# Loading and splitting weights in two phases of a one-core hybrid decoder step

## The chip, the cores and the metric

The kernel runs on one core of one Trainium2 chip. The metric is the device time of one execution in microseconds (us). Three runs of the kernel before took 3761.02, 3762.74 and 3765.28 us, so the median is 3762.74 us.

Engine names in the profile: PE is the matrix engine (PEld its weight loads), DVE the vector engine, ACT the scalar engine, POOL the general engine; SP issues the DMAs that matter here, and SPq is its queue. A time such as 2690.67 is in microseconds from the first instruction of the profiled execution.

## The reference

One layer of a decoder. A prompt of 4096 tokens and 32 sample tokens (8 sequences of 4) are normalised and projected by `w_in` into a pooling group (`u`, gate) and an attention group (q, k, v, gate, forget logits). The part that matters here is what stands behind attention:

```python
z = jnp.einsum('btd,de->bte', h, w_in_l)            # u_pool, g_pool, q, k, v, g_attn, logits
...
outs.append((end[..., sl] - start) / cnt - uf[..., sl])   # mean over 2, 4, 8, 16 tokens, minus the token
mixed = jnp.einsum('btgc,gcd->btgd', pooled, pool_w_l) * pool_scale_l
...
mix = jnp.concatenate([pool_out * jax.nn.silu(g_pool),
                       attn_out.reshape(b, t, ATTN_W) * jax.nn.silu(g_attn)], axis=-1)
return x + jnp.einsum('bte,ed->btd', mix, w_out_l)  # then a final RMSNorm
```

Everything is float32. A product of two float32 matrices is made of three matmuls: each operand is split into a high part, which is a rounded copy, and a low part, which is the operand minus that copy, and high x high, high x low and low x high are added up in PSUM.

## The kernel before, in words

Five phases follow each other, each with its own buffers and semaphores and with a barrier of all engines between them: project, decode (attention of the sample tokens over the cache), attend (prompt), gates (`phase_gates`, L1093) and merge (`phase_merge`, L1419). The change touches the last two.

**Gates** computes `u` and the two gates, for 512 prompt tokens (a super tile) at a time, eight times. First it needs its weights: 8 chunks of 128 rows x 1536 columns (`w_in`, 768 KB each in two DMAs). SP loads a chunk into one of two raw slots, which lie in the buffer of the later output stage (L1177, L1178). ACT scales it by the norm weight and rounds it to `w_high` (L1236), DVE makes `w_low` (L1278), and that frees the slot for the chunk after the next. PE multiplies each finished chunk with the 32 sample tokens (three columns of 512, three passes: 9 matmuls a chunk, 72 in all). Behind chunk 1 SP also issues the first `h_t` (2 MB, the tokens of the first super tile), the pooling weights, the history and `den`.

Behind the last chunk stands the sample chain: DVE inverts `den` (L1282) and splits the pooling weights; ACT copies and applies the sigmoid to the sample results (L1240, L1242); PE makes 8 small matmuls for the pooled sample tokens (L1381, L1382), DVE copies them, PE makes 4 more (L1386, 8 records in the trace), and DVE multiplies the gates (L1304 to L1308). Then DVE splits the first `h_t` into `h_high` and `h_low` in 8 chunks (L1292, L1293), and PE begins the first super tile.

A super tile has 12 groups of output columns (u = 0 to 11), each of 8 chunks x 3 passes = 24 matmuls of 128x128 by 512; ACT evacuates or applies a sigmoid, DVE makes sums, gates and the next `h_t` split. Three PSUM banks `acc` rotate over the groups. Group u = 11 closes a super tile; DVE then splits the next `h_t`, and PE waits for its first chunk. All eight super tiles are one loop on PE (`Fori`).

**Merge** loads `w_out` in 8 chunks of 128 x 1024 (512 KB, L1494) into two raw slots; DVE alone rounds (L1558) and subtracts (L1559). Behind chunk 1 stand the sample's inputs and `norm_row`. PE turns the sample's mix around, multiplies it chunk by chunk (6 matmuls a chunk, 48 in all) into `acc`, and DVE adds and normalises it (L1598, L1600). SP issues behind the last weight chunk the first half super tile of inputs (`load_mix(0, 0)`: four loads of 512 KB and two of 256 KB, L1480 and L1482), then x (1 MB), then the same for the second half. DVE joins the inputs and splits them (`split_mix`, L1575 to L1581). PE waits until DVE has added the sample result (`s_done` 2) before it starts the loop over eight super tiles of four token tiles t, 48 matmuls each. In the loop SP loads the mix for half b of the next super tile when DVE has freed the buffer, but in program order behind the store of y and the load of x of the other half.

## Time and profile before

| what | us |
|---|---|
| median of three runs | 3762.74 |
| the profiled execution's own time | 3761.75 |
| its span, first to last instruction | 3760.2 |
| PE busy in the span | 3457.5 (92%) |
| from 2680, end of attend, to the first matmul of the first super tile of gates | 55.6 |
| one super tile of gates | 76 |
| from the last transpose of gates (3341.4) to the first token tile of merge | 51.9 |

The profiled execution is one run of its own; its time stands 1.0 us below the median of the three. The page's busy shares are means over phases with different limits, so the stretches in question are read by themselves from the timeline. A figure in square brackets at the end of a timeline row is how long that engine had been idle, and what it waited for.

### The profile page before, as it was taken

The numbers are of one execution on the slowest core, as the hardware profiler recorded it, in microseconds if no ns is written. First come the engines' busy times: TensorE is split into PE (matmuls) and PEld (weight loads), VectorE is DVE, ScalarE is ACT, GpSimd is POOL, SyncE is SP. The second block draws the span as 40 slices with busy tenths as digits, with TensorE's granted clock in tenths as the row PEclk, the third lists the DMA queues.
The fourth block names the chain that finished last, engine by engine and source line by source line (L and its number), as shares of the span: only waits on it lengthen the run. The fifth ranks groups of instructions, "written<-read, shape, count | busy, mean of one in ns | idle before, by whom it ended". The sixth has DMA issues, their size and how long they took to land. (4 is left out here: it accounts for less than half of the span.)

```text
span 3760.2 us, 51171 instructions
## 1 busy us (share of the span) xinstructions
PE 3457.5 (92%) x18808; PEld 2382.5 (63%) x18808; DVE 1709.7 (45%) x2714; ACT 1176.0 (31%) x1611; POOL 1198.2 (32%) x1145
## 2 busy tenths in 40 slices
PE   7999999797948999999999999999799999979998
PEld 5777777573715555655565656565377777757887
DVE  3222221262526655555555555555243444445554
ACT  4221121141314455555555555554301000000100
POOL 0000000134324666666666666666400000000000
PEclk9999999897978999999999999999899999989999
DMA  4222232499983020202020212100311111136765
GB/s 149 90 101 101 103 121 81 159 347 388 335 303 73 18 54 21 57 23 57 23 57 23 55 25 52 29 21 9 103 49 67 45 56 56 45 110 185 212 209 163
DMA packets 216028, 392.73 MB, mean 104 GB/s; under 512 B 60135, under 2 KB 102120, under 8 KB 213775
## 3 DMA queue, kind: packets, MB, share of 16 engines
q1 hardware_dynamic: 195079, 322.22, 27.6%
q0 software_dynamic: 20768, 68.17, 4.8%
q8 instruction: 105, 1.72, 0.2%
q14 instruction: 76, 0.62, 0.0%
HBM read 288.50 MB, written 101.99 MB: 104 GB/s over the span
## 5 line engine op out<-in xcount | busy, mean ns | idle before, releaser
L928 DVE TENSOR_REDUCE at_max_parts<-at_mx 128x1 f32<-128x512 f32 (+3 forms) x1152 | 731.0, 645 | 494.9 <-PE at_mx L997 425.4
L802 POOL TENSOR_TENSOR at_pair_sum<-at_probs 128x1024 f32<-128x1024 f32 x224 | 532.0, 2375 | 424.3 <-ACT at_probs L852 424.3
L852 ACT ACTIVATE at_probs<-at_st,at_gap 128x1024 f32<-128x1024 f32 x448 | 498.0, 1113 | 523.1 <-PE at_st L1029 516.2
L1049 PE MATMUL at_o_ps<-at_probs,at_v 128*64 128x512 f32 (+3 forms) x2304 | 541.8, 581 | 0.0
L1028 PE MATMUL at_st<-at_q_all,at_k_all 128*128 128x512 f32 (+3 forms) x1152 | 476.4, 414 | 0.0
L997 PE MATMUL at_mx<-at_k_one,at_q_top 67*128 67x512 f32 (+3 forms) x1152 | 453.5, 395 | 8.7 <-DVE at_max_parts L928 5.9
L1029 PE MATMUL at_st<-at_q_one,at_k_one 67*128 67x512 f32 (+3 forms) x1152 | 439.2, 381 | 0.0
L1028 PEld LDWEIGHTS at_st<-at_q_all,at_k_all 128*128 128x128 f32 x1152 | 217.8, 189 | 224.6 <-ACT at_probs L852 115.2
L93 PE MATMUL ga_acc<-ga_h_high,ga_w_high 128*128 128x512 f32 x768 | 312.0, 406 | 22.9 <-DVE ga_h_low L1293 21.3
L95 PE MATMUL ga_acc<-ga_h_high,ga_w_low 128*128 128x512 f32 x768 | 308.4, 402 | 0.0
L94 PE MATMUL ga_acc<-ga_h_low,ga_w_high 128*128 128x512 f32 x768 | 308.3, 401 | 0.0
L803 POOL TENSOR_TENSOR at_quad_sum<-at_pair_sum 128x512 f32<-128x512 f32 x224 | 287.8, 1285 | 17.6
L1049 PEld LDWEIGHTS at_o_ps<-at_probs,at_v 128*64 128x64 f32 x2304 | 146.3, 138 | 208.5 <-issue 156.8
L997 PEld LDWEIGHTS at_mx<-at_k_one,at_q_top 67*128 67x128 f32 x1152 | 219.7, 191 | 64.8 <-DVE at_max_parts L928 17.1
L1029 PEld LDWEIGHTS at_st<-at_q_one,at_k_one 67*128 67x128 f32 x1152 | 220.4, 191 | 30.2
L93 PE MATMUL mg_acc<-mg_w_high,mg_mix_high 128*128 128x512 f32 x512 | 201.0, 393 | 22.0 <-DVE mg_xs L1598 17.1
L93 PE MATMUL pj_acc<-pj_h_high,pj_w_high 128*128 128x512 f32 x512 | 209.6, 409 | 6.2 <-DVE pj_fs L430 6.2
L1522 POOL MEMSET mg_minus_half<- 128x1 f32 x1 | 0.1, 99 | 656.0 <-POOLq L66 656.0
L95 PE MATMUL pj_acc<-pj_h_high,pj_w_low 128*128 128x512 f32 x512 | 206.1, 403 | 0.0
L94 PE MATMUL pj_acc<-pj_h_low,pj_w_high 128*128 128x512 f32 x512 | 205.6, 402 | 0.0
L94 PE MATMUL mg_acc<-mg_w_low,mg_mix_high 128*128 128x512 f32 x512 | 200.4, 391 | 0.0
L95 PE MATMUL mg_acc<-mg_w_high,mg_mix_low 128*128 128x512 f32 x512 | 200.1, 391 | 0.0
(305 smaller groups left out, 4926.1 us busy)
## 6 DMA issues: line engine op xcount, KB each, us to landing
dc_pages<-in_cache_k_dram SPq DMA_DIRECT2D x128, 256.0 KB, 5.2
dc_pages<-in_cache_k_dram POOLq DMA_DIRECT2D x128, 256.0 KB, 5.2
dc_pages<-in_cache_v_dram SPq DMA_DIRECT2D x128, 256.0 KB, 7.1
dc_pages<-in_cache_v_dram POOLq DMA_DIRECT2D x128, 256.0 KB, 5.4
pj_x<-in_x_prompt_dram SPq DMA_DIRECT2D x32, 512.0 KB, 3.8
scratch_h_t<-pj_h_t SPq DMA_DIRECT2D x8, 2048.0 KB, 10.1
at_q_raw<-scratch_q_t SPq DMA_DIRECT2D x128, 128.0 KB, 3.0
at_k_raw<-scratch_k_t SPq DMA_DIRECT2D x64, 256.0 KB, 4.1
```

The lines of the kernel that those rows point to most:

```text
L93: nc.tensor.matmul(out, lhs_high, rhs_high, start=first, stop=False)
L94: nc.tensor.matmul(out, lhs_high, rhs_low, start=False, stop=False)
L95: return nc.tensor.matmul(out, lhs_low, rhs_high, start=False, stop=last)
L802: chain.link(nc.gpsimd.tensor_tensor(pair, first, second, ALU.add))
L803: nc.gpsimd.tensor_tensor(out, pair[:, 0], pair[:, 1], ALU.add).then_inc(summed, 1)
L852: nc.scalar.activation(probs[:, s % RING], st[:, s % 2], ACT.Exp, bias=bias).then_inc(exp_done, 1)
L928: nc.vector.tensor_reduce(max_parts[:, b % AHEAD, t, c:c + 1], mx[:, bank_of["unit", k] % 2, 0:width], AX_X, ALU.max).then_inc(bank_done, 1)
L997: last = nc.tensor.matmul(mx[:, n % 2, 0:width], q_top[0:KR, b % AHEAD, t * P:(t + 1) * P], k_one[h % 2][0:KR, c * TILE:c * TILE + width], ...
L1028: nc.tensor.matmul(out, k_all[h % 2][:, keys], q_all[:, b % AHEAD, at:TILE], start=True, stop=False)
L1029: last = nc.tensor.matmul(out, k_one[h % 2][0:KR, keys], q_one[0:KR, b % 2, at:TILE], start=False, stop=(c < j))
L1049: last = nc.tensor.matmul(o_ps[half * HD:(half + 1) * HD, b % 2, at:TILE], v[:, h % 2, 4 * c + own], probs[:, s % RING, half, at:TILE], st ...
L1522: nc.gpsimd.memset(minus_half[:], -0.5)
```

## The change

In gates there are four raw slots in place of two: three in a larger stage buffer, one in `u_t`. `norm_col` and `den` are loaded first, then the weights, with `h_t` behind chunk 5 and the other constants behind chunk 7. The inversion of `den` stands ahead of the weights on DVE. ACT makes the first `h_high` (8 copies) behind the last `w_high`, DVE only the subtractions. The sample's projections go to a PSUM tile `side` of their own, and the rest of the sample chain moves into the first super tile, which is now written out ahead of the loop: the 8 small matmuls ahead of u = 10, the 4 others behind u = 11, DVE's part between its gates.

In merge all eight chunks have a slot of their own, ACT rounds them and DVE subtracts. `load_mix(0, 0)` is issued behind chunk 4 and `norm_row` behind chunk 7; DVE runs `split_mix(0, 0)` between chunks 4 and 5. The sample's result goes to the other `acc` buffer, and PE waits for its addition only ahead of t = 1 of the first super tile, written out too.

```diff
--- before.py
+++ after.py
...
-INVERTED = 7
+INVERTED = 3
+PW_SPLIT = 9
 BANDS_READY = 10
-LAST_COPY = 15
+LAST_COPY = 13
...
+    WSLOTS = 4
...
+        stage = m.sb("stage", [P, 2 * CH + 2, TILE])
+        pool_stage, gate_stage, sig = stage[:, 0:CH], stage[:, CH:2 * CH], stage[:, 2 * CH:2 * CH + 2]
...
+        w_raw = [flat[:, 0:NW], flat[:, NW:2 * NW], flat[:, 2 * NW:3 * NW], u_t[:].rearrange("p c t -> p (c t)")[:, 0:NW]]
...
+        side = m.ps("side", [P, 3, W])
+        s_acc, s_mixed, last_ps = side[0:NS], side[0:NS, 0], side[0:HIST, 1]
+        s_ps = side[:, 0, 0:CH * NS].rearrange("p (g t) -> p g t", g=CH)
...
+            sp.dma_start(norm_col[:], io["norm_w"].rearrange("l (c p) -> p (l c)", p=P), allow_slow_non_contiguous=True).then_inc(norm_loaded, 16)
+            sp.dma_start(den, io["den"].rearrange("h (a t) -> (h a) t", t=DEN)).then_inc(den_loaded, 16)
+            for c in range(KC):
+                if c >= WSLOTS:
+                    sp.wait_ge(w_low_dve, c - WSLOTS + 1)
+                rows = w_in[c * P:(c + 1) * P]
+                slot = w_raw[c % WSLOTS]
+                sp.dma_start(slot[:, 0:2 * W], rows[:, U0:U0 + 2 * W]).then_inc(w_loaded[c % WSLOTS], 16)
+                sp.dma_start(slot[:, 2 * W:NW], rows[:, GA0:GA0 + W]).then_inc(w_loaded[c % WSLOTS], 16)
+                if c == 5:
+                    sp.dma_start(h_t[:], io["h_t"][0]).then_inc(h_loaded, 16)
+            sp.dma_start(pw_raw[:], io["pool_w"].rearrange("l g c d -> c (l g) d")).then_inc(const_loaded, 16)
+            sp.dma_start(hist[:], io["state_pool"].rearrange("l b i c -> (l b i) c")).then_inc(const_loaded, 16)
             sp.dma_start(scale_col[:], io["pool_scale"].rearrange("l (c p) -> p (l c)", p=P), allow_slow_non_contiguous=True).then_inc(const_loaded, 16)
             sp.dma_start(scale_row[:], io["pool_scale"].to_broadcast([NS, W])).then_inc(const_loaded, 16)
-            for c in range(KC):
-                if c >= 2:
-                    sp.wait_ge(w_low_dve, c - 1)
-                rows = w_in[c * P:(c + 1) * P]
-                slot = w_raw[:, (c % 2) * NW:(c % 2 + 1) * NW]
-                sp.dma_start(slot[:, 0:2 * W], rows[:, U0:U0 + 2 * W]).then_inc(w_loaded[c % 2], 16)
-                sp.dma_start(slot[:, 2 * W:NW], rows[:, GA0:GA0 + W]).then_inc(w_loaded[c % 2], 16)
-                if c == 1:
-                    sp.dma_start(h_t[:], io["h_t"][0]).then_inc(h_loaded, 16)
-                    sp.dma_start(pw_raw[:], io["pool_w"].rearrange("l g c d -> c (l g) d")).then_inc(const_loaded, 16)
-                    sp.dma_start(hist[:], io["state_pool"].rearrange("l b i c -> (l b i) c")).then_inc(const_loaded, 16)
-                    sp.dma_start(den, io["den"].rearrange("h (a t) -> (h a) t", t=DEN)).then_inc(den_loaded, 16)
             sp.wait_ge(setup, INVERTED)
             sp.dma_start(io["inv_den"].rearrange("h (a t) -> (h a) t", t=DEN), den).then_inc(inv_stored, 16)
...
+            act.wait_ge(norm_loaded, 16)
             for c in range(KC):
-                act.wait_ge(w_loaded[c % 2], 32 * (c // 2 + 1))
-                nc.scalar.activation(w_high[:, c], w_raw[:, (c % 2) * NW:(c % 2 + 1) * NW], ACT.Copy, scale=norm_col[:, c:c + 1]).then_inc(w_high_ready, 1)
+                act.wait_ge(w_loaded[c % WSLOTS], 32 * (c // WSLOTS + 1))
+                nc.scalar.activation(w_high[:, c], w_raw[c % WSLOTS], ACT.Copy, scale=norm_col[:, c:c + 1]).then_inc(w_high_ready, 1)
+            act.wait_ge(h_loaded, 16)
+            for c in range(KC):
+                nc.scalar.activation(h_high[:, c], h_t[:, c], ACT.Copy).then_inc(h_high_first, 1)
...
             dve.wait_ge(den_loaded, 16)
             link(nc.vector.reciprocal(den, den))
             assert n_setup[0] == INVERTED
-            dve.wait_ge(const_loaded, 80)
+            dve.wait_ge(norm_loaded, 16)
+            for c in range(KC):
+                dve.wait_ge(w_high_ready, c + 1)
+                nc.vector.scalar_tensor_tensor(out=w_low[:, c], in0=w_raw[c % WSLOTS], scalar=norm_col[:, c:c + 1],
+                                               in1=w_high[:, c].bitcast(F32), op0=ALU.mult, op1=ALU.subtract).then_inc(w_low_dve, 1)
+            for c in range(KC):
+                dve.wait_ge(h_high_first, c + 1)
+                nc.vector.tensor_tensor(h_low[:, c], h_t[:, c], h_high[:, c].bitcast(F32), ALU.subtract).then_inc(h_split.sem, 1)
+            dve.wait_ge(w_low_dve, KC)
+            for g in range(CH):
+                link(nc.vector.memset(u_t[:, g, 0:HALO], 0.0))
+            dve.wait_ge(const_loaded, 64)
             link(nc.vector.tensor_copy(pw_high[:], pw_raw[:]))
             link(nc.vector.tensor_tensor(pw_low[:], pw_raw[:], pw_high[:].bitcast(F32), ALU.subtract))
...
-            dve.wait_ge(s_pooled, 1)
-            link(nc.vector.tensor_copy(pooled_s[:], s_ps[:]))
...
-            dve.wait_ge(s_pooled, 3)
-            link(nc.vector.tensor_tensor(keep["mix_s"][:, 0:W], mixed[0:NS, 0], sig_s[:, 0], ALU.mult))
-            nc.vector.nop().then_inc(s_pooled, 1)
-
-            first = Chain(dve, dve_chain)
-            split_h(0, first)
+            def sample_gates():
+                dve.wait_ge(bands, 7 * CH)
+                for g in range(CH):
+                    last = nc.vector.tensor_tensor(band_new[:, g], band_new[:, g], keep["ident"][0:NS, 0:NS], ALU.subtract)
+                link(last)
+                assert n_setup[0] == BANDS_READY
+                dve.wait_ge(s_sig, 3)
+                nc.vector.tensor_tensor(sig_s[:, 0], s_acc[:, 1], sig_s[:, 0], ALU.mult).then_inc(s_gated, 1)
+                nc.vector.tensor_tensor(keep["mix_s"][:, W:D], s_acc[:, 2], sig_s[:, 1], ALU.mult).then_inc(s_gated, 1)
+                dve.wait_ge(s_gated, 2)
+                nc.vector.tensor_tensor(sig_s[:, 0], sig_s[:, 0], scale_row[:], ALU.mult).then_inc(s_gated, 1)
+
+            def sample_pooled():
+                dve.wait_ge(s_pooled, 1)
+                link(nc.vector.tensor_copy(pooled_s[:], s_ps[:]))
+
+            def sample_mix():
+                dve.wait_ge(s_pooled, 2)
+                dve.wait_ge(s_gated, 3)
+                link(nc.vector.tensor_tensor(keep["mix_s"][:, 0:W], s_mixed, sig_s[:, 0], ALU.mult))
+
             dve.wait_ge(inv_stored, 16)
-            base = first.n
-
-            def super_tile(s, more):
-                chain = Chain(dve, dve_chain, s * (PER + KC) + base)
+
+            def super_tile(s, more, first=False):
+                chain = Chain(dve, dve_chain, s * (PER + KC))
...
+                if first:
+                    sample_gates()
                 for c in range(CH):
                     k = CH + c
+                    if first and c == 2:
+                        sample_pooled()
+                    if first and c == CH - 1:
+                        sample_mix()
                     if c == 0:
                         dve.wait_ge(gate_stored, s * 16 + 16)
...
-            with dve.Fori(0, NT - 1) as s:
+            super_tile(0, True, True)
+            with dve.Fori(1, NT - 1) as s:
...
-            pe.wait_ge(setup, BANDS_READY)
-            pe.wait_ge(s_sig, 1)
-            for g in range(CH):
...
-            pe.wait_ge(setup, BANDS_READY + 1)
...
-            pe.wait_ge(s_pooled, 4)
-
...
+            def super_tile(s, first=False):
                 for u in range(3 * CH):
+                    if first and u == 3 * CH - 2:
+                        sample_pool()
                     if u < 3:
...
                         g = u - CH - 1
+                        if first:
+                            pe.wait_ge(setup, PW_SPLIT)
...
-            with pe.Fori(0, NT) as s:
+                    if first and u == 3 * CH - 1:
+                        sample_mix()
+
+            super_tile(0, True)
+            with pe.Fori(1, NT) as s:
                 super_tile(s)
...
-        w_raw = m.sb("w_raw", [P, 2, D])
+        w_raw = m.sb("w_raw", [P, KC, D])
...
-            for c in range(KC):
-                if c >= 2:
-                    sp.wait_ge(w_split, c - 1)
-                sp.dma_start(w_raw[:, c % 2], io["w_out"][0, c * P:(c + 1) * P]).then_inc(w_loaded[c % 2], 16)
-                if c == 1:
-                    sp.dma_start(attn_s[:], io["attn_s"]).then_inc(const_loaded, 16)
-                    sp.dma_start(xs[:], io["x_sample"].rearrange("b t d -> (b t) d")).then_inc(const_loaded, 16)
-                    sp.dma_start(norm_row[:], io["norm_f"].rearrange("(a d) -> a d", a=1).to_broadcast([P, D])).then_inc(const_loaded, 16)
-            for b in range(2):
-                load_mix(0, b)
-                load_x(0, b)
+            def load_w(c):
+                sp.dma_start(w_raw[:, c], io["w_out"][0, c * P:(c + 1) * P]).then_inc(w_loaded[c], 16)
+
+            for c in range(2):
+                load_w(c)
+            sp.dma_start(attn_s[:], io["attn_s"]).then_inc(const_loaded, 16)
+            sp.dma_start(xs[:], io["x_sample"].rearrange("b t d -> (b t) d")).then_inc(const_loaded, 16)
+            for c in range(2, 5):
+                load_w(c)
+            load_mix(0, 0)
+            for c in range(5, KC):
+                load_w(c)
+            sp.dma_start(norm_row[:], io["norm_f"].rearrange("(a d) -> a d", a=1).to_broadcast([P, D])).then_inc(norm_loaded, 16)
+            load_x(0, 0)
+            load_mix(0, 1)
+            load_x(0, 1)
             sp.wait_ge(s_ready, 1)
             sp.dma_start(io["y_sample"].rearrange("b t d -> (b t) d"), xs[:]).then_inc(s_stored, 16)
...
+            for c in range(KC):
+                act.wait_ge(w_loaded[c], 16)
+                nc.scalar.activation(w_high[:, c], w_raw[:, c], ACT.Copy).then_inc(w_high_ready, 1)
...
-            for c in range(KC):
-                dve.wait_ge(w_loaded[c % 2], 16 * (c // 2 + 1))
-                start.link(nc.vector.tensor_copy(w_high[:, c], w_raw[:, c % 2]))
-                nc.vector.tensor_tensor(w_low[:, c], w_raw[:, c % 2], w_high[:, c].bitcast(F32), ALU.subtract).then_inc(w_split, 1)
-                if c == 1:
-                    dve.wait_ge(const_loaded, 48)
-                    start.link(nc.vector.tensor_tensor(keep["mix_s"][:, W:D], keep["mix_s"][:, W:D], attn_s[:], ALU.mult))
...
+            def low_part(c):
+                dve.wait_ge(w_high_ready, c + 1)
+                nc.vector.tensor_tensor(w_low[:, c], w_raw[:, c], w_high[:, c].bitcast(F32), ALU.subtract).then_inc(w_split, 1)
+
+            low_part(0)
+            dve.wait_ge(const_loaded, 32)
+            start.link(nc.vector.tensor_tensor(keep["mix_s"][:, W:D], keep["mix_s"][:, W:D], attn_s[:], ALU.mult))
+            nc.vector.nop().then_inc(s_split, 1)
+            low_part(1)
+            dve.wait_ge(s_turned, 1)
+            start.link(nc.vector.tensor_copy(ms_high[:], s_ps[:]))
+            nc.vector.tensor_tensor(ms_low[:], s_ps[:], ms_high[:].bitcast(F32), ALU.subtract).then_inc(s_split, 1)
+            for c in range(2, 5):
+                low_part(c)
 
...
             split_mix(0, 0, Chain(dve, dve_chain))
-
+            for c in range(5, KC):
+                low_part(c)
+
+            dve.wait_ge(norm_loaded, 16)
+            start.link(nc.vector.tensor_scalar(norm_row[:], norm_row[:], ROOT_D, None, ALU.mult))
             dve.wait_ge(s_done, 1)
-            nc.vector.tensor_tensor(xs[:], acc[0:NS, 0], xs[:], ALU.add).then_inc(s_done, 1)
...
+                    last = three_pass(nc, acc[0:NS, 1, cols], ms_high[:, c], ms_low[:, c], w_high[:, c, cols], w_low[:, c, cols],
...
             last.then_inc(s_done, 1)
-            pe.wait_ge(s_done, 2)
-
-            with pe.Fori(0, NT) as g:
+
+            def super_tile(g, first=False):
                 for t in range(TT):
+                    if first and t == 1:
+                        pe.wait_ge(s_done, 2)
...
+
+            super_tile(0, True)
+            with pe.Fori(1, NT) as g:
+                super_tile(g)
```

## Rows read from the trace of the kernel before

**Rows 1.** The page, part 1: busy time, share of the span, instructions.
```profile
PE 3457.5 (92%) x18808; PEld 2382.5 (63%) x18808; DVE 1709.7 (45%) x2714; ACT 1176.0 (31%) x1611; POOL 1198.2 (32%) x1145
```

**Rows 2.** Windows: length, busy (count) by engine, PEclk, DMA share, GB/s.
```profile
2680.00:2736.00 56.00, 28.30 (x121) 13.25 (x110) 23.52 (x56) 15.54 (x12) 6.03 (x28) 0.74 0.53 171
...
2692.00:2696.00 4.00, 1.74 (x5) 0.72 (x6) 3.22 (x2) 1.82 (x2) 0.50 (x2) 0.50 0.99 417
...
2696.00:2700.00 4.00, 4.00 (x11) 1.67 (x10) 0.42 (x1) 0.00 (x0) 0.00 (x0) 0.50 1.02 310
...
3344.00:3393.00 49.00, 14.72 (x56) 6.67 (x56) 25.73 (x28) 0.00 (x0) 0.13 (x2) 0.65 0.82 245
...
3437.50:3482.00 44.50, 44.50 (x198) 36.86 (x197) 24.25 (x22) 4.61 (x8) 2.97 (x8) 1.00 0.70 204
```

**Rows 3.** Waits, gates then merge: total us, times, longest.
```profile
PE ga_acc L93 <- DVE ga_w_low L1278: 23.5, 6, 13.7
...
PE mg_acc L93 <- DVE mg_xs L1598: 17.1, 1, 17.1
```

**Rows 4.** Timeline of ACT and DVE, start of gates: start, us, instruction, idle before.
```profile
2690.67 1.57 ACT L1236 ACTIVATE ga_w_high<-ga_stage,ga_norm_col 128x1536 fp32r<-128x1536 f32 x1 [12.93 <-DMA ga_stage<-in_w_in_dram]
...
2702.35 1.57 ACT L1236 ACTIVATE ga_w_high<-ga_stage,ga_norm_col 128x1536 fp32r<-128x1536 f32 x1 [7.79 <-DMA ga_stage<-in_w_in_dram]
...
2720.95 1.58 ACT L1236 ACTIVATE ga_w_high<-ga_stage,ga_norm_col 128x1536 fp32r<-128x1536 f32 x1 [1.33 <-DMA ga_stage<-in_w_in_dram]
...
2722.56 1.82 DVE L1278 SCALAR_TENSOR_TENSOR ga_w_low<-ga_stage,ga_norm_col,ga_w_high 128x1536 fp32r<-128x1536 f32 x1 [1.09 <-ACT ga_w_high L1236]
...
2734.78 0.69 DVE L1293 TENSOR_TENSOR ga_h_low<-ga_h_t,ga_h_high 128x512 fp32r<-128x512 f32 x1
...
2744.12 0.60 ACT L1249 ACTIVATE ga_u_t<-ga_acc 128x512 f32<-128x512 f32 x1 [15.81 <-PE ga_acc L95]
```

**Rows 5.** Timeline of PE, start of gates.
```profile
2694.26 0.63 PE L93 MATMUL ga_acc<-ga_w_high,keep_hs_high 128*32 128x512 f32 x1 [13.66 <-DVE ga_w_low L1278]
...
2700.24 0.43 PE L95 MATMUL ga_acc<-ga_w_high,keep_hs_low 128*32 128x512 f32 x1
...
2705.83 0.64 PE L93 MATMUL ga_acc<-ga_w_high,keep_hs_high 128*32 128x512 f32 x1 [4.47 <-DVE ga_w_low L1278]
...
2727.81 0.41 PE L1381 MATMUL ga_s_ps<-ga_band_hist,ga_hist 120*128 120x32 f32 x2 [1.10 <-DVE ga_band_new L1298]
...
2731.02 1.91 PE L1386 MATMUL ga_mixed<-ga_pw_raw,ga_pooled_s 128*32 128x128 f32 x8 [0.45 <-DVE ga_pooled_s L1302]
...
2735.61 0.77 PE L93 MATMUL ga_acc<-ga_h_high,ga_w_high 128*128 128x512 f32 x1 [2.68 <-DVE ga_h_low L1293]
```

**Rows 6.** Timeline of DVE, then PE, start of merge.
```profile
3352.18 0.69 DVE L1558 CAST mg_w_high<-mg_w_raw 128x1024 fp32r<-128x1024 f32 x1 [8.56 <-DMA mg_w_raw<-in_w_out_dram]
...
3372.67 0.69 DVE L1558 CAST mg_w_high<-mg_w_raw 128x1024 fp32r<-128x1024 f32 x1 [1.29 <-DMA mg_w_raw<-in_w_out_dram]
...
3384.55 1.23 DVE L1575 TENSOR_TENSOR mg_raw<-mg_raw 128x1024 f32<-128x1024 f32 x1 [9.93 <-DMA mg_raw<-scratch_inv_den]
...
3391.81 1.21 DVE L1598 TENSOR_TENSOR mg_xs<-mg_acc,mg_xs 32x1024 f32<-32x1024 f32 x1
...
3393.35 0.79 PE L93 MATMUL mg_acc<-mg_w_high,mg_mix_high 128*128 128x512 f32 x1 [17.10 <-DVE mg_xs L1598]
```

**Rows 7.** Timeline of merge: DVE, then SP's queue.
```profile
3416.95 1.23 DVE L1588 TENSOR_TENSOR mg_x<-mg_acc,mg_x 128x1024 f32<-128x1024 f32 x1 [6.23 <-PE mg_acc L95]
...
3427.83 1.23 DVE L1588 TENSOR_TENSOR mg_x<-mg_acc,mg_x 128x1024 f32<-128x1024 f32 x1 [1.20 <-PE mg_acc L95]
...
3431.57 0.37 SPq L1480 DMA_DIRECT2D mg_raw<-scratch_pool_t  x1
...
3705.39 0.37 SPq L1480 DMA_DIRECT2D mg_raw<-scratch_pool_t  x1
```

**Rows 8.** DMA queues, 3345 to 3400: packets, MB, share of 16 engines.
```profile
q8 instruction: 1, 0.02, 0.1%
```

81 lines of the change are left out of this document (31 added, 50 removed).

## The prediction

> **What bounds the kernel now.** The page's busy shares come first: PE is busy for 92% of the span [rows 1]. So a change away from PE can only matter where PE stands still. The windows by stage say where that is: 56 us at the start of gates hold 28.3 us of PE, and 49 us at the start of merge hold 14.7, while merge in its stride has all of its time [rows 2]. The waits name the causes: PE waited 23.5 us for the low parts of the weights in gates, and 17.1 us in one piece for the sample addition in merge [rows 3]. Last the timelines of the two starts, for what ends each wait.
>
> In gates, ACT's first chunk lands at 2690.67, the third 11.7 us later [rows 4]: chunk 1, `h_t`, the pooling weights, the history, `den` and chunk 2 lie between, 4.31 MB by the kernel's shapes, so 369 GB/s. That is transfer-bound. From there on each chunk waits for a slot to come free, and DVE's last low part ends at 2722.56 + 1.82 = 2724.4 [rows 4]. Then comes the serial sample chain and `h_t`'s split, and PE's first super tile starts at 2735.61 [rows 5], at half clock; its first group is evacuated at 2744.12 [rows 4].
>
> In merge the last weight chunk is there at 3372.67, the first mix at 3384.55, 11.9 us later; `split_mix` takes 7.3 us to 3391.81, and the sample addition stands behind it, so PE starts at 3393.35 [rows 6].
>
> **Gates, the weights.** The bytes don't change, their order and the waits do. With four slots SP is always two or more chunks ahead: a slot is held for ACT's 1.6 and DVE's 1.8 us, overlapped from chunk to chunk [rows 4], and a chunk takes 0.786 MB / 369 GB/s = 2.1 us to land. I put the first landing at 2690.3 (two small loads fewer ahead of it, `den` more). Seven chunks and `h_t` behind it are 7.60 MB, 20.6 us: chunk 7 at 2710.9. ACT and DVE behind it, 1.58 + 1.82 + some 0.2: w_low complete at 2714.5 in place of 2724.4. The inversion of `den`, 1.75 us of DVE work by the same timeline, now runs before the first chunk is there, in time that DVE idles. Bounds of the rate: 310 and 417 GB/s, two 4 us windows of this stretch with the queues full [rows 2]; they move the end by +3.9 and -2.4 us.
>
> PE's 72 sample matmuls start at half clock, 0.43 us each from 2694.26 to 2700.24 [rows 5], then take 0.23. They keep up until chunk 5 (done near 2709) and wait for chunk 6, which `h_t` has pushed back, until about 2712.4. After an idle 4.47 us the clock was at half again [rows 5]; the new gap is 3.4 us, so I leave both open: the projections end at 2716.6 at full, 2718.9 at half clock. I take 2718.
>
> **Gates, the first tokens.** ACT makes `h_high` behind w_high 7 (8 x 0.60, the price of a 128x512 ACT copy, to 2717.7), DVE subtracts 8 x 0.69 at most from 2714.5, to 2720.0 [rows 4]. PE needs a chunk each 0.70 us from 2718, so it is never late. The first group of 24 ends 5.6 us after 2718, at 2723.6, not at 2744.1, for it isn't paced by DVE and the clock is up. That is 20.5 us. Half of it is the weights, the rest is the sample chain and the split.
>
> **Gates, what comes back.** The chain's matmuls are still PE work: 8 products from 2727.81 to about 2730.6, 2.75 us, then 1.91 us [rows 5]. The first stand ahead of u = 10, where PE is the bound: 2.75 us in full. The second stand behind u = 11, where PE idles 2.7 us anyway for DVE's split; but DVE waits for them before its last gate, and its product (0.7 us) is in line too, while ACT's sigmoid runs beside it. The split of the next tokens comes some 1.9 us later, and PE with it. DVE's other sample work (four small subtractions, three products, 2.7 us) stands after its fourth pooling gate; the next thing due on PE from there is bank 2 for u = 11, two groups or 11 us later, so it costs nothing. PE's new wait for the pooling weights' split is met: DVE has it by about 2722, it is asked for at u = 5. Gates: 20.5 - 2.75 - 1.9 = 15.9 us, bounds 12 and 19.
>
> **Merge.** With all slots there SP waits for nothing. From the first chunk at 3352.18 [rows 6], four more and the two sample inputs (2.3 MB at 369 GB/s, 6.2 us) have landed by 3358.4. The first mix behind them: before, it took 11.9 us from the last weight chunk to its landing [rows 6], which is slower than its 2.6 MB at 369 GB/s (7.1 us), as its rows are 1 KB and one of its sources is read 64 times. I take 11.9, so 3370.3. `split_mix` 7.3 us, to 3377.6; meanwhile chunks 5 to 7 land and ACT rounds them (1.1 us each, between its 0.60 for 512 and 1.58 for 1536 columns [rows 4]). DVE subtracts chunk 5 by 3378.9, then two more. PE stood still since chunk 4, so its last 18 sample matmuls begin at half clock: eight to fourteen of them slow, 5.8 to 6.9 us, end at 3385.3. The token tiles follow directly, with the clock up. Before, they started at 3393.35 and lost 1.6 us to the slow clock (8 matmuls at 0.43 in place of 0.23), in effect 3394.9. Gain 9.6 us.
>
> The addition, the norm and `norm_row`'s scaling are now beside t = 0, which PE takes 10.9 us for (3416.95 to 3427.83 is one tile [rows 7]). The second half's mix lands near 3390, its split ends by 3400, PE asks at 3385.3 + 2 x 10.9 = 3407: met.
>
> Bounds for merge: if the first mix shares the queue with chunks 5 to 7 behind it, it lands 1.57 MB / 369 GB/s = 4.3 us later, gain 5.3; at full rate it lands 4.8 us earlier, gain 14.4. The Trainium skill (DMA: Bandwidth & Descriptors, "Queues, rings and completion order") says that descriptors are taken up in ring order on each DMA engine while completion is not first in, first out for the issuing engine. By its first half the sum stands, by its second merge gives 5.3 us; no run here has weights issued behind an unfinished mix.
>
> **Does merge's loop give it on?** The mix for b = 1 is issued at 3431.57 and, six super tiles on, at 3705.39: 45.6 us each [rows 7], though PE needs only 4 x 10.9 = 43.5. So the loop is set by SP's chain of store, load and mix, not by PE. But this chain starts from PE's second tile (DVE's addition at 3416.95, then the split, then the store), and shifts with it. The next mix is issued behind the sample's store, near 3391, and must be there by the addition at 3409; it needs about 12 us. The gain passes through if this holds.
>
> **Sum.** 15.9 + 9.6 = 25.5 us off the profiled execution's 3761.75: 3736.2. The median of the runs is 1.0 us higher, so 3737.
>
> **Rivals.**
> 1. Merge returns its gain: the mix lands late among the weights, or the next one is late for the loop. For: the loop is set by transfers. Against: 18 us of room. Only gates' gain is left, some 2 us with it: 3745.
> 2. More than I say: both transfers at their fast bound and the clock up throughout, 19 + 14: 3729.
> 3. Both starts are worth little, as PE's gaps are filled by another late thing (the chain's end in u = 11, `inv_stored` ahead of DVE's first pooling sums, which is queued behind all loads). For: that store is now issued near 2703 behind 0.6 MB of constants. Against: it lands before 2716 even so and is wanted at 2724. 8 to 12 us off: 3752.
> 4. Slower: the tiles written out ahead of the loops make PE fetch some 1000 more instructions at the two moments at which the data queue is deepest. If a fetch stood behind the queued data, each would cost up to the 11.9 us of a mix; from three such fetches on the gain is gone, and four make 3763 + 48 - 25 = 3785. Against: one instruction packet passed in the busiest 55 us of merge with no wait of PE for it [rows 8], and attend is long unrolled code. The Trainium skill (same page, "Queues, rings and completion order", on arbitration) has each DMA engine take turns between queues packet by packet; by that rule a fetch waits for one packet, and this rival is worth nothing.
>
> **How the numbers follow.** The forecast 0.62, rival 1 0.14, rival 2 0.08, rival 3 0.10, rival 4 0.05, and 0.01 for a change that does nothing. The forecast's own range is 12 + 5.3 to 19 + 14.4 less, narrowed to 3731 to 3744, as the bounds hardly fall together. The range on record reaches into rivals 1 to 3: 3728 to 3750. A measurement tells 0.2%, 7.5 us, from no change. Faster by more (below 3755.2): all of the forecast, of rivals 1 and 2 and nearly all of 3, 0.93; within it 0.03; slower 0.04.
>
> **What would show it.** In the changed profile: ACT's eight `w_high` without gaps except one of about 6 us for `h_t` ahead of chunk 6; the last w_low near 2714; the first `ga_u_t` evacuation near 2724; 2.7 us of small matmuls in the first super tile and a boundary 1.9 us longer behind it; in merge a PE start some 25 us earlier than 3393 on the clock of the span, `split_mix` starting 22 us after the phase's first load, and the 45.6 us cadence kept. The forecast is wrong if gates' first group ends later than 2729, if the first mix lands beside chunk 7, or if DVE's split of the second super tile in merge waits for its mix.

## The result, and the profile after

| | us |
|---|---|
| before, median of 4 runs on the same chip | 3764.01 |
| changed, median of 4 runs | 3734.21 (3732.40 to 3741.80) |
| ratio of changed to before | 0.9924, 95% interval 0.9906 to 0.9941 |
| the profiled execution of the changed kernel | 3741.80, its span 3740.2 |

The forecast was 3737 us, 25.5 us off the profiled execution. The medians differ by 29.8 us; the two profiles by 20.0. Both figures carry scatter of the phases ahead of gates, so the phases were measured by themselves. In the table, "end of attend" is the start of DVE's last copy of attend (L944), "gates" runs from there to SP's first load of merge, "merge" from there to the last instruction. All figures are read from the timelines and worked out by subtraction, in us.

| profile | end of attend | last w_low starts | first group evacuated | next h_t load | gates | first mix at DVE | first add of x | merge | gates + merge |
|---|---|---|---|---|---|---|---|---|---|
| before | 2680.7 | 41.9 | 63.5 | 138.5 | 667.7 | 36.2 | 57.7 | 411.8 | 1079.5 |
| changed | 2684.8 | 33.5 | 44.4 | 124.7 | 654.1 | 22.4 | 48.6 | 401.3 | 1055.4 |

(Columns 3 to 5 count from the end of attend, 7 and 8 from merge's first load.) So the changed phases are 13.6 + 10.5 = 24.1 us shorter, and attend ended 4.1 us later in this one execution, although nothing ahead of gates is changed.

PE's work is the same as before [rows 1]; the page's first line of the changed kernel:

```profile
PE 3455.9 (92%) x18808; PEld 2382.3 (64%) x18808; DVE 1700.7 (45%) x2698; ACT 1188.6 (32%) x1627; POOL 1197.1 (32%) x1145
```

What is left of PE's wait for the weights in gates, total, times and longest (before: 23.5 in six pieces [rows 3]); it contains the 14.2 us ahead of the first chunk, about what before has there (13.7):

```profile
PE ga_side L93 <- DVE ga_w_low L1287: 18.0, 2, 14.2
```

The same for merge. The 17.1 us for the sample's addition [rows 3] are gone; in their place stand 12.8 us ahead of chunk 5, whose low part DVE makes behind the mix's split; the second row is the loop's wait, which before has as well:

```profile
PE mg_acc L93 <- DVE mg_w_low L1599: 12.8, 1, 12.8
PE mg_acc L93 <- DVE mg_x L1630: 4.3, 2, 2.4
```

The start of gates: ACT's chunks 0, 6 and 7, DVE's last w_low, PE's chunk 6 and first super tile, the first evacuation. They answer to [rows 4, 5]:

```profile
2695.34 1.57 ACT L1242 ACTIVATE ga_w_high<-ga_stage,ga_norm_col 128x1536 fp32r<-128x1536 f32 x1 [13.45 <-DMA ga_stage<-in_w_in_dram]
...
2714.21 1.57 ACT L1242 ACTIVATE ga_w_high<-ga_stage,ga_norm_col 128x1536 fp32r<-128x1536 f32 x1 [5.50 <-DMA ga_stage<-in_w_in_dram]
...
2716.70 1.57 ACT L1242 ACTIVATE ga_w_high<-ga_u_t,ga_norm_col 128x1536 fp32r<-128x1536 f32 x1 [0.92 <-DMA ga_u_t<-in_w_in_dram]
...
2718.31 1.82 DVE L1287 SCALAR_TENSOR_TENSOR ga_w_low<-ga_u_t,ga_norm_col,ga_w_high 128x1536 fp32r<-128x1536 f32 x1 [0.67 <-ACT ga_w_high L1242]
...
2717.69 0.64 PE L93 MATMUL ga_side<-ga_w_high,keep_hs_high 128*32 128x512 f32 x1 [3.86 <-DVE ga_w_low L1287]
...
2723.32 0.39 PE L93 MATMUL ga_acc<-ga_h_high,ga_w_high 128*128 128x512 f32 x1
...
2729.19 0.60 ACT L1258 ACTIVATE ga_u_t<-ga_acc 128x512 f32<-128x512 f32 x1 [3.90 <-PE ga_acc L95]
```

ACT waits 5.5 us for chunk 6, behind `h_t`, as forecast; PE had been idle for 3.86 us and ran the first seven matmuls of it at half clock (granted share 0.50, the lower of the two levels, 1.2 and 2.4 GHz): a record then lasts 0.64 us in place of 0.40, and they start 0.43 us apart in place of 0.23. The last w_low ends 35.3 us behind the end of attend, not at 43.7, PE goes straight into the first super tile, and its first group is evacuated 19.1 us earlier.

In the first super tile, the small products ahead of u = 10 (one row, then the u = 10 matmuls behind them), the products behind u = 11, and the start of the next super tile:

```profile
2782.80 0.30 PE L1403 MATMUL ga_side<-ga_band_hist,ga_hist 120*128 120x32 f32 x2
...
2785.39 0.51 PE L93 MATMUL ga_acc<-ga_h_high,ga_w_high 128*128 128x512 f32 x1
...
2786.12 0.63 PE L95 MATMUL ga_acc<-ga_h_high,ga_w_low 128*128 128x512 f32 x1
...
2798.32 1.06 PE L1410 MATMUL ga_side<-ga_pw_raw,ga_pooled_s 128*32 128x128 f32 x8
...
2802.05 0.48 PE L93 MATMUL ga_acc<-ga_h_high,ga_w_high 128*128 128x512 f32 x1 [2.67 <-DVE ga_h_low L1304]
```

The start of merge: ACT's chunks 0, 4 and 5, DVE's split and addition, PE's chunk 5 and first token tile. They answer to [rows 6]:

```profile
3342.30 1.06 ACT L1582 ACTIVATE mg_w_high<-mg_w_raw 128x1024 fp32r<-128x1024 f32 x1 [9.52 <-DMA mg_w_raw<-in_w_out_dram]
...
3348.71 1.06 ACT L1582 ACTIVATE mg_w_high<-mg_w_raw 128x1024 fp32r<-128x1024 f32 x1 [0.26 <-DMA mg_w_raw<-in_w_out_dram]
...
3362.39 1.06 ACT L1582 ACTIVATE mg_w_high<-mg_w_raw 128x1024 fp32r<-128x1024 f32 x1 [12.62 <-DMA mg_w_raw<-in_w_out_dram]
...
3361.33 1.22 DVE L1617 TENSOR_TENSOR mg_raw<-mg_raw 128x1024 f32<-128x1024 f32 x1 [10.02 <-DMA mg_raw<-scratch_inv_den]
...
3375.65 1.21 DVE L1644 TENSOR_TENSOR mg_xs<-mg_acc,mg_xs 32x1024 f32<-32x1024 f32 x1 [2.97 <-PE mg_acc L95]
...
3369.86 0.64 PE L93 MATMUL mg_acc<-mg_w_high,mg_ms_high 128*32 128x512 f32 x1 [12.79 <-DVE mg_w_low L1599]
...
3375.38 0.40 PE L93 MATMUL mg_acc<-mg_w_high,mg_mix_high 128*128 128x512 f32 x1
```

The first mix is split 22.4 us behind the first load at 3338.93, where before took 36.2 (3348.40 to 3384.55). The split takes 7.3 us, chunk 5's low part 1.2, the 18 sample matmuls 5.5 (half clock for the first seven), and the token tiles start at 36.5, where before's started at 45.0 and at half clock.

### The profile page after: what moved, and what is told of

Read it like the earlier page. It is cut to its first block and busy times, and to the rows that moved or that the text cites. A ratio compares the mean times of both kernels' runs of the same rounds, so it can differ in the third digit from the quotient of the medians.

```text
span 3740.2 us, 51105 instructions
## 1 busy us (share of the span) xinstructions
PE 3455.9 (92%) x18808; PEld 2382.3 (64%) x18808; DVE 1700.7 (45%) x2698; ACT 1188.6 (32%) x1627; POOL 1197.1 (32%) x1145
```

## The experiments

All are edits of the changed kernel unless said otherwise. Two more profiles of before and of the changed kernel came with them; the table collects all. The ratio is to before, timed on the same chip.

| kernel | median of runs | ratio (95%) | end of attend | gates | merge | gates + merge |
|---|---|---|---|---|---|---|
| before, second profile | 3762.80 | 1.0002 (0.9992 to 1.0011) | 2678.9 | 667.2 | 411.5 | 1078.7 |
| changed, second profile | 3740.88 | 0.9930 (0.9917 to 0.9943) | 2680.6 | 654.4 | 404.1 | 1058.4 |
| gates_only | 3745.53 | 0.9943 (0.9930 to 0.9955) | 2678.3 | 654.2 | 412.4 | 1066.6 |
| merge_only | 3752.05 | 0.9959 (0.9946 to 0.9972) | 2676.2 | 667.7 | 403.6 | 1071.3 |
| h_last | 3736.48 | 0.9923 (0.9909 to 0.9936) | 2682.6 | 647.6 | 404.4 | 1052.0 |
| slots_two | 3745.79 | 0.9952 (0.9935 to 0.9969) | 2683.9 | 660.8 | 402.1 | 1062.9 |
| chain_back | 3747.68 | 0.9962 (0.9948 to 0.9976) | 2677.6 | 660.5 | 408.4 | 1068.9 |
| h_dve | 3737.17 | 0.9932 (0.9914 to 0.9951) | 2678.7 | 654.2 | 403.9 | 1058.1 |
| add_first | 3739.31 | 0.9939 (0.9922 to 0.9956) | 2677.8 | 651.8 | 406.3 | 1058.1 |
| best | 3729.14 | 0.9907 (0.9889 to 0.9925) | 2680.6 | 647.3 | 402.2 | 1049.4 |
| mix_ahead | 3734.02 | 0.9926 (0.9908 to 0.9943) | 2681.2 | 652.0 | 394.3 | 1046.3 |
| best_ahead | 3726.51 | 0.9905 (0.9888 to 0.9922) | 2679.6 | 646.3 | 393.1 | 1039.4 |

**Each phase alone, and both again.** The changed `phase_gates` with the old `phase_merge`, the reverse, and the changed kernel once more.

> The changed gates phase with merge as before. Theory: each phase's gain is PE time that stood still at its own start, and the two add up. In the profile of the changed kernel, counted from the end of attend, gates brings 13.6 us and merge 10.5. So this kernel is 13.6 us faster than before (0.9964), and its merge phase lasts as long as before's. Rival: the measured 29.8 us are 5 more than the 24.1 that the two phases show, because the change does something to the phases it does not touch (other addresses, other code); then this kernel is 16 to 19 us faster, or the surplus sits in merge alone. Second rival: gates' gain is eaten in merge, 5 us or less.

> The changed merge phase with gates as before. Theory: 10.5 us faster than before (0.9972), the first mix 22 us behind the phase's first load, PE's first token tile 36.7 us behind it. Rival that the surplus of 5 us sits here: 15 us faster. Rival that merge's loop, paced by SP's chain of store and load, gives the early start back: 3 us or less.

> The changed kernel once more. Theory: 24 us faster than before, as its two phases show, and the 29.8 us of the medians were partly the scatter of decode and attend, which the change leaves alone: ratio 0.9936, give or take 0.001. Rival: the surplus is real, 30 us (0.992), and is found in the phases before gates, which then end earlier than before's 2678.6 in most profiles.

In the profiles the two are separate: gates is 667.7 or 654.2 with either merge, merge 412.4 or 403.6 with either gates. So neither gives anything back to the other. The profiles bear out the theory for gates and come in 2.3 us under it for merge (8.2 us where 10.5 were expected). The medians don't: they give 22.4 us for gates alone, 15.9 for merge alone and 27.1 for both, against a median of before of 3768 us in that set. The parts add up to more than the whole, which no place in the traces explains. Against the median of all runs of before, 3764.0, the three are 18.5, 12.0 and 23.1 us, which still add up to more.

**Before once more.** The same kernel, unchanged.

> The kernel before, once more, for a second profile of it. The changed kernel's own phases are 22 to 24 us shorter than before's, but the medians differ by 27 to 30. Theory: the rest is scatter of decode and attend, which the change leaves alone; the end of attend stood at 2676 to 2685 us in the five profiles so far, whatever the kernel. Then this profile has gates at 667.7 us and merge at 412 again, within 1 us, and only the end of attend moves. Rival: the first profile of before was a lucky one, and gates or merge (its loop, which is paced by transfers) last 4 us longer in most executions.

Gates and merge repeat to within 0.5 us, so the rival of a lucky first profile has nothing for it. The end of attend lay between 2676.2 and 2684.8 in 14 profiles, with no order by kernel, which is 8.6 us of scatter in phases that are the same in all. Merge scatters too: its changed form as it stands was profiled seven times and took 401.3 to 408.4 us, 404.0 in the mean, beside 411.5 to 412.4 for the old one in three profiles (mean 411.9). The scatter sits in its loop: PE's token tiles, from first to last, take 355.0 to 359.8 us, of which PE waits 4.3 to 7.1, while what follows them takes 9.8 us in every profile. Over all 47 runs of before the median is 3764.0, over the nine of the changed kernel 3740.6: 23.4 us, beside 22.2 for gates and merge in the mean of two profiles each. Sets of four or five runs can miss by several us. Where in decode or attend the scatter arises was not looked into.

**The order of `h_t`.**

```diff
-                if c == 5:
+                if c == KC - 1:
                     sp.dma_start(h_t[:], io["h_t"][0]).then_inc(h_loaded, 16)
```

> The changed kernel with the first h_t loaded behind chunk 7 instead of chunk 5. Theory: PE's wait of 3.9 us ahead of chunk 6 and the half clock behind it (8 matmuls, 1.6 us) come from h_t in the queue; without it the last w_low ends near 32 us behind the end of attend instead of 37.3, the sample projections end there + 2, and the first super tile waits for h_t alone, which lands as late as chunk 7 did (33.5): PE starts near 36, not 40.5, so 3 to 5 us faster than the changed kernel. Rival: transfers are the bound whatever their order, and ACT's and DVE's h split now stands behind all transfers, so PE starts at 40 and nothing changes (within 1 us).

ACT's chunk 7 and its first copy of `h_t`, and PE's first super tile:

```profile
2707.91 1.58 ACT L1242 ACTIVATE ga_w_high<-ga_u_t,ga_norm_col 128x1536 fp32r<-128x1536 f32 x1 [0.68 <-DMA ga_u_t<-in_w_in_dram]
...
2713.07 4.28 ACT L1245 ACTIVATE ga_h_high<-ga_h_t 128x512 fp32r<-128x512 f32 x8 [3.57 <-DMA ga_h_t<-scratch_h_t]
...
2714.57 0.47 PE L93 MATMUL ga_acc<-ga_h_high,ga_w_high 128*128 128x512 f32 x1 [0.82 <-DVE ga_h_low L1291]
```

The gap of 5.5 us is gone (ACT's longest between two chunks is now 1.7 us), PE never falls back to half clock in the projections, and the first super tile starts 32.0 us behind the end of attend instead of 38.5. The gain is 6.6 us of gates, above the 3 to 5 expected: `h_t` landed 30.5 us behind the end of attend, three earlier than I had put the last transfer. The rival (only the sum of the bytes counts) is out: the order matters, because ACT's and DVE's work on the weights now runs under `h_t`'s transfer.

**Two slots.**

```diff
-    WSLOTS = 4
+    WSLOTS = 2
```

> The changed kernel with two raw slots in gates instead of four. Theory: a chunk can be asked for only when DVE has finished the one two before it, and needs 4.1 us from issue to landing, so the chunks come in pairs 8 us apart as before: the last w_low ends 8 to 10 us later than in the changed kernel, and gates is 8 to 10 us longer. Rival: the order of the loads (h_t behind chunk 5, the constants last) is what helps, and the slots give little: 0 to 3 us longer.

ACT's chunks 1 to 4:

```profile
2696.36 1.57 ACT L1242 ACTIVATE ga_w_high<-ga_stage,ga_norm_col 128x1536 fp32r<-128x1536 f32 x1 [0.25 <-DMA ga_stage<-in_w_in_dram]
...
2702.43 1.58 ACT L1242 ACTIVATE ga_w_high<-ga_stage,ga_norm_col 128x1536 fp32r<-128x1536 f32 x1 [4.49 <-DMA ga_stage<-in_w_in_dram]
...
2705.45 1.58 ACT L1242 ACTIVATE ga_w_high<-ga_stage,ga_norm_col 128x1536 fp32r<-128x1536 f32 x1 [1.44 <-DMA ga_stage<-in_w_in_dram]
...
2710.26 1.58 ACT L1242 ACTIVATE ga_w_high<-ga_stage,ga_norm_col 128x1536 fp32r<-128x1536 f32 x1 [3.24 <-DMA ga_stage<-in_w_in_dram]
```

Chunk 2 comes 6 us behind chunk 1, chunk 4 nearly 8 behind chunk 2: pairs, as forecast. Gates is 6.6 us longer than with four slots. That is under the 8 to 10 expected and well over the 0 to 3 of the rival: of the 13.3 us that gates gained (667.5 to 654.2, each the mean of three profiles), half hang on the slots. The last w_low starts at 40.1, so of the 8 us by which it had moved the new order alone keeps under 2.

**The sample chain back ahead of the first super tile.**

```diff
+            sample_gates()
+            sample_pooled()
+            sample_mix()
             super_tile(0, True, True)
...
+            sample_pool()
+            sample_mix()
             super_tile(0, True)
             with pe.Fori(1, NT) as s:
```

with the calls inside the super tile taken out.

> The changed kernel with the sample chain back ahead of the first super tile, on PE and on DVE; all else as changed. Theory: PE then waits at the end of the projections for the small products (2.75 and 1.9 us) and for DVE and ACT between them (the sample results' copy, the bands, the pooled copy): the first super tile starts 8 to 10 us later and is 5.0 us shorter, since it no longer holds them: gates 4 us longer (658), the whole 4 us slower. Rival: moving the chain bought nothing, since its matmuls are still PE work (within 1 us).

PE's small products in this kernel, and the windows over them (length, busy and count by engine, PEclk, DMA share, GB/s):

```profile
2719.85 0.41 PE L1400 MATMUL ga_side<-ga_band_hist,ga_hist 120*128 120x32 f32 x2 [3.84 <-DVE ga_band_new L1310]
...
2724.55 1.91 PE L1407 MATMUL ga_side<-ga_pw_raw,ga_pooled_s 128*32 128x128 f32 x8 [0.38 <-DVE ga_pooled_s L1321]
```

```profile
2716.00:2720.00 4.00, 0.16 (x3) 0.15 (x2) 3.65 (x14) 1.98 (x3) 0.00 (x0) 1.00 0.23 49
2720.00:2724.00 4.00, 4.00 (x16) 3.57 (x16) 1.78 (x3) 0.00 (x0) 0.00 (x0) 0.53 0.88 350
2724.00:2728.00 4.00, 3.62 (x13) 2.59 (x14) 0.97 (x2) 0.00 (x0) 0.00 (x0) 0.50 0.35 147
2728.00:2732.00 4.00, 4.00 (x14) 3.15 (x13) 0.00 (x0) 0.00 (x0) 0.00 (x0) 0.69 0.00 0
```

Gates is 6.3 us longer; 4 were expected. The first super tile starts 10 us later and is 5.2 shorter from its first evacuation to the next load of `h_t`, as the theory says; most of the rest is the clock, for the first group took 7.9 us from its first matmul to its evacuation where the changed kernel takes 5.9. PE had been idle for 3.84 us, then did small products, and the clock stood at half (PEclk 0.53, 0.50) until deep in the first group. Inside the super tile they have matmuls on both sides. Merge, which this edit doesn't touch, was 408.4 in this profile, 4 us over the highest of the six others: PE's first token tile came 38.8 us behind the first load, where the others have 36.2 to 36.9, and PE waited 7.1 us in the loop, where they have 4.3 to 5.6. Why is not known.

**The split by DVE alone.**

```diff
-            act.wait_ge(h_loaded, 16)
-            for c in range(KC):
-                nc.scalar.activation(h_high[:, c], h_t[:, c], ACT.Copy).then_inc(h_high_first, 1)
...
+            dve.wait_ge(h_loaded, 16)
             for c in range(KC):
+                nc.vector.tensor_copy(h_high[:, c], h_t[:, c]).then_inc(h_high_first, 1)
                 dve.wait_ge(h_high_first, c + 1)
```

> The changed kernel with the first h_t split by DVE alone, copy and subtraction by turns, 1.06 us a chunk in place of 0.61. Theory: PE starts the first super tile when the sample projections end, which is 3.2 us behind DVE's last w_low; DVE's pace of 1.06 against PE's 0.70 uses this up by the last chunk only, so the first group ends 0.5 to 1 us later. The second engine brings next to nothing here. Rival: the split is what the first group's end hung on, 3 us later (the difference of 8.5 and 5.6 us that before's first group shows).

The first group was evacuated at 45.2, in the two profiles of the changed kernel at 44.4 and 45.0, and gates is 654.2 as with two engines. The second engine brings nothing measurable in the changed kernel, where the split runs beside the projections. What taking the split out of the way was worth by itself no run shows.

**The wait for the sample's addition.**

```diff
-                    if first and t == 1:
+                    if first and t == 0:
                         pe.wait_ge(s_done, 2)
```

> The changed kernel in which PE waits for the sample's addition ahead of t = 0 of merge, not t = 1. Theory: the addition is 1.2 us of DVE, free at that moment, so PE's first token tile starts 1.3 to 1.5 us later and merge is that much longer: the wait that the profile of before charged with 17.1 us was the mix's, whose split stood ahead of the addition. Rival: the wait itself was the price, and the kernel loses over 4 us.

PE's first token tile:

```profile
3367.67 0.50 PE L93 MATMUL mg_acc<-mg_w_high,mg_mix_high 128*128 128x512 f32 x1 [1.38 <-DVE mg_xs L1644]
```

It starts after 1.38 us of idling, 38.1 us behind the first load, where the changed kernel has 36.5. Merge was 406.3, 2 to 5 over the changed kernel's two profiles but inside the scatter, so only the start can be told. The theory holds there, and the edit that the profile of before seemed to ask for (17.1 us of waiting [rows 3]) is worth 1.5 us; the rest of the 17.1 was time in which the mix was on its way or being split.

**The first mix behind all weights, and `h_t` last (best).** SP issues all eight chunks and then `load_mix(0, 0)`; DVE makes all low parts ahead of `split_mix(0, 0)`; `h_t` as in h_last.

```diff
-            for c in range(2, 5):
-                load_w(c)
-            load_mix(0, 0)
-            for c in range(5, KC):
+            for c in range(2, KC):
                 load_w(c)
+            load_mix(0, 0)
```

> The changed kernel with h_t behind chunk 7 in gates (6.5 us earlier start of the first super tile, as the kernel with that edit alone showed) and in merge the first mix behind all eight weight chunks, all low parts ahead of its split. For merge the theory is that the queue is served in order: the mix lands 3 to 4 us later (25 to 27 us behind the phase's first load instead of 22), but the sample's matmuls are all done by then, so PE starts right behind the split, 34 us behind the first load instead of 36.7, at half clock for 3.5 us: merge within 1 us of the changed kernel or 1 us better, in all 6 to 8 us faster than the changed kernel. Rival: the early mix is what merge's gain came from, and PE starts at 40 us: 3 us lost in merge.

ACT's chunk 7, DVE's split, PE's first token tile, with merge's first load at 3327.81:

```profile
3342.47 1.06 ACT L1580 ACTIVATE mg_w_high<-mg_w_raw 128x1024 fp32r<-128x1024 f32 x1 [0.35 <-DMA mg_w_raw<-in_w_out_dram]
...
3352.99 1.22 DVE L1615 TENSOR_TENSOR mg_raw<-mg_raw 128x1024 f32<-128x1024 f32 x1 [8.20 <-DMA mg_raw<-scratch_inv_den]
...
3360.39 0.79 PE L93 MATMUL mg_acc<-mg_w_high,mg_mix_high 128*128 128x512 f32 x1 [9.83 <-DVE mg_mix_low L1621]
```

The mix is there 25.2 us behind the first load, 2.8 later than in the changed kernel, and PE starts at 32.6, 3.9 earlier but at half clock. In merge as a whole that is 402.2, within the scatter of the changed merge (401.3 to 408.4): no difference told. In kernels whose loop doesn't make PE wait (mix_ahead and best_ahead, below) the same step brings 1.2 us, 394.3 to 393.1: PE starts 4.0 earlier and loses 2.7 to the slow clock. So placing the mix among the weights rather than behind them is not what merge gained by; what is left of its edits is that the loads no longer wait for buffers, that ACT does the rounding, and that PE no longer waits for the sample's addition (1.5 us in add_first). The first two no run here took back alone.

**The loop of merge.** SP issues both mixes as soon as the buffers are free; since a store no longer stands between, the wait is for `mix_ready`, which DVE raises at the same place as `raw_free`, behind the last low part.

```diff
                 for b in range(2):
-                    sp.wait_ge(raw_free[b], g + 1)
+                    sp.wait_ge(mix_ready.sem, mix_ready.at(g, b + 1))
                     load_mix(g + 1, b)
+                for b in range(2):
                     store_y(g, b)
```

> The changed kernel with SP's loop in merge reordered: both mixes of the next super tile are issued as soon as DVE has split the present ones, ahead of the stores of y and the loads of x. Theory of the prediction: the loop is set by SP's chain of store, load and mix (45.6 us a super tile where PE needs 43.5), so DVE's waits for the mix in the loop (75 to 82 us in all kernels so far) nearly vanish, PE's waits of 4 to 6 us too, and merge is 5 to 8 us shorter. Rival: the transfers of a super tile fill the DMA engines anyway (share 0.7 on the mean, over 1 where the mix lands), and the cadence stays; within 2 us.

DVE's wait for the mix from 3400 to the end (total, times, longest), first in the changed kernel, then with this edit:

```profile
DVE mg_raw L1617 <- DMA mg_raw<-scratch_inv_den: 74.8, 13, 10.3
```

```profile
DVE mg_raw L1618 <- DMA mg_raw<-scratch_inv_den: 16.9, 6, 4.2
```

Two late super tiles of each, first the changed kernel:

```profile
3576.00:3620.00 44.00, 42.19 (x186) 34.62 (x185) 22.84 (x21) 3.99 (x8) 2.96 (x8) 1.00 0.69 201
3620.00:3664.00 44.00, 41.55 (x182) 34.09 (x181) 22.90 (x22) 4.45 (x8) 2.22 (x6) 0.99 0.67 196
```

```profile
3599.00:3643.00 44.00, 44.00 (x196) 36.44 (x195) 24.64 (x23) 4.61 (x8) 2.95 (x8) 1.00 0.75 219
3643.00:3687.00 44.00, 44.00 (x196) 36.44 (x195) 24.64 (x23) 4.60 (x8) 2.95 (x8) 1.00 0.69 220
```

PE has no gap left in these two, and SP issues a super tile's loads every 43.5 us in place of 45.6, with the DMA engines about as busy as before (share 0.75 and 0.69, beside 0.69 and 0.67), so on the mean they were not full; the chain of store, load and mix on SP set the cadence. Merge is 394.3, 9.7 us shorter than the mean of the changed merge in seven profiles (404.0) and 7 below the lowest of them. PE's token tiles take 348.4 us from first to last, against 355.0 and 357.5 in the two profiles of the changed kernel: 4.3 and 5.0 of the difference are PE's waits, which are gone, and most of the rest is the half clock behind them. The mechanism is as expected, the gain at or above the 5 to 8 us (7.0 and 9.8 beside those two profiles).

**All together (best_ahead).** h_last, the first mix last, and mix_ahead.

> All that helped in one kernel: h_t behind chunk 7 in gates, the first mix behind all weights in merge, and SP's loop in merge issuing both mixes as soon as they are free. Theory: the gains stand at different places and add: gates 647.5 (6.5 us off the changed kernel's 654), merge 393 to 394 (9 off its 403): 15 us faster than the changed kernel, 38 to 40 faster than before (0.990). Rival: an earlier start of the loop makes PE overtake the mixes again, and merge stays at 397 or more.

Gates and merge take 1039.4 us, 39.7 less than the mean of before's two profiles and 17.5 less than the changed kernel's two. Its ratio to before, 0.9905 (0.9888 to 0.9922), is the lowest of all; the interval overlaps that of best and of the changed kernel. The medians of its set differ by 33.4 us, under the 38 to 40 expected, which the phases do show.

## Why the prediction was right

**Gates, weights.** The last w_low was to move 9.9 us and moved 8.4 (7.5 in the second profile). I had written that with four slots SP is always two or more chunks ahead, and it is not. SP can ask for chunk 4 only when DVE has made chunk 0's low part; by then little was left in the queue, and ACT waited for the chunk:

```profile
2698.90 0.33 SPq L1182 DMA_DIRECT2D ga_stage<-in_w_in_dram  x1
...
2705.13 1.58 ACT L1242 ACTIVATE ga_w_high<-ga_stage,ga_norm_col 128x1536 fp32r<-128x1536 f32 x1 [2.46 <-DMA ga_stage<-in_w_in_dram]
```

In the two us from 2699 the DMA engines moved 266 and 207 GB/s, where the two before had 426 and 401; the second profile has the same hole (256 and 188 GB/s, ACT idle for 2.60 us). Behind it the queue was full, and `h_t` and chunk 6, 2.88 MB, took 7.1 us, 407 GB/s. So the 7.60 MB from chunk 0 to chunk 7 took 21.4 us, 356 GB/s where I had used 369, only because a hole that I did not foresee and a rate above mine nearly cancel. That part of the agreement is luck, and what a fifth slot would bring was not tested. The first chunk was 0.5 us later than in before, not 0.4 earlier; h_last, with the same loads ahead of it, has it 0.5 earlier, so that is scatter. slots_two shows that the slots carry most of what the weights gained.

**Gates, first tokens.** The first group was forecast 20.5 us earlier; it came 18.4 to 19.1 earlier. Chunk 6 began at half clock, the later of the two cases that I left open. Of the 19.1 us of the first profile 8.4 are the weights, 8.1 the stretch from the last w_low's end to PE's first matmul of the super tile (11.3 to 3.2), and 2.6 the first group itself. chain_back puts the sample chain at 10.3 us of delay to the start of the super tile. For the last part I had named two causes, DVE's pace and the clock. In before's trace the 24 matmuls of that group follow each other without a gap, the first half of them 0.43 us apart and the rest 0.23, and chain_back, whose split was long done, still took 7.9 us for the group with the clock at half. So in those runs it was the clock. But DVE had the last chunk of the split ready at 2742.91 and PE used it at 2743.38, so with the clock up DVE's pace would have held before's group almost as long: both had to go.

**Gates, what comes back.** Forecast 2.75 + 1.9 = 4.65 us; the first super tile grew by 5.3 between evacuation and next load (75.1 to 80.3) in seven of the ten profiles with the chain in it, and by 3.7 in the other three. The 1.6 us between them are the clock, below. Net 13.3 us where 15.9 were forecast, within the bounds of 12 and 19.

**Merge.** Forecast 9.6; the profiles give 10.5 and 7.6 for the changed kernel, 7.9 is the mean over the seven profiles with this merge (404.0 beside 411.9). The sum was made for the stage's start, and there it is right: PE's first token tile was to come 36.9 us behind the first load and came at 36.5. What is missing at the end are the 1.6 us that I added because the tiles now start with the clock up: from first to last they take 357.3 us in the mean of the seven, as in the three profiles of the old merge (357.4), for the loop takes it back: PE waits 5.3 us in it beside 4.9, and behind its waits it has 3.4 to 6.8 us at half clock where the old merge has 3.4. So the gain passes through, but not the whole of it. The first mix was to land at 21.9 us and did at 21.4 to 22.7 (23.6 in chain_back); the queue did serve weights, mix and weights in order: ACT got chunk 5 at 3362.39, 1.1 us behind DVE's start on the mix. So the bound of 5.3 us, by which the mix shares the queue with what is behind it, did not come about. Here the Trainium skill (DMA: Bandwidth & Descriptors, "Queues, rings and completion order") states that completion need not follow the order of issue; in this trace the landings did follow it, 22.4 and 23.5 us behind the first load.

**The loop.** That it is set by SP's chain and that the chain shifts with PE was right in both parts: mix_ahead and merge_only show them, and the cadence of 45.6 us was kept. The split that begins the second super tile had no wait for its mix, as asked; its second half waited 2.73 us, as before's did (2.46). I didn't see that the chain itself was worth as much as merge's whole change (9.7 beside 7.9 us).

**The rivals.** Rival 1 (merge gives its gain back) is refuted by merge_only. Rival 2 needed the clock up throughout, and chunk 6's first matmuls were at half clock, as were the first seven behind the mix in merge. Rival 4 (code loading) is refuted by the first super tiles, in which PE has no wait but those named; the page counts 109 instruction packets where before had 105. Rival 3's store of `inv_den` was issued at 2713.2 and held up nothing: DVE began the first sums 0.1 us behind the evacuation.

**The total** of 25.5 us is 3.3 above what the phases show in two profiles each (22.2), and lies among what the medians give (29.8 and 27.1 in the two sets, 23.4 over all runs). Over all profiles of each phase gates was over-forecast by 2.6 us and merge by 1.7. That the first median hit the forecast so closely is in part luck.

## What to carry to other kernels

A wait in the profile is charged to the last instruction ahead of it: ask what that one had waited for. Here the 17.1 us against "the sample's addition" were spent behind a 12 us transfer and a 7 us split, and moving the wait alone was worth 1.5. Where weights arrive by DMA and are split behind, count when each slot comes free again: four slots in place of two were worth 6.6 us in gates and still left one hole of 2.5 us. What isn't needed until later can go behind all weights: 6.6 us for `h_t` in gates, no difference for the mix in merge. In a loop whose busiest engine has nearly no idle time, still check the queue's order: here loads behind a store gave SP a round of 45.6 us where PE needs 43.5, PE's lead was used up and it waited in the late super tiles, and moving the loads ahead was the largest gain of a single edit in this stage.
